# Linear half of the experts' first bias: from a TensorE matmul to a row read back from DRAM and added by VectorE

## What is computed

```python
def expert_block(args):
    xblk, e = args
    hh = xblk @ w1[e] + b1[e]                      # 1024 -> 2048
    glu = jnp.minimum(hh[:, :D_FF], SWIGLU_LIMIT)  # the gate's half
    lin = jnp.clip(hh[:, D_FF:], -SWIGLU_LIMIT, SWIGLU_LIMIT)  # the linear half
    act = glu * jax.nn.sigmoid(SWIGLU_ALPHA * glu) * (lin + 1.0)
    return act @ w2[e] + b2[e]
```

## Time and profile before

| what | value |
|---|---|
| median of 3 runs | 2273.63 us |
| the profiled execution, its own time | 2272.34 us |
| its span, from the first to the last instruction | 2270.5 us |
| granted TensorE clock, mean | 0.997 |
| TensorE busy | 98% of the span |
| VectorE busy | 78% of the span |
| ScalarE busy | 55% of the span |
| bytes moved by DMA | 542.98 MB |

### The profile page before, as it was taken

One profiled execution on the slowest core, in us unless ns is written; L12 is line 12 of the kernel. 1 busy time (PEld: TensorE's weight loads), 2 busy tenths in 40 slices (PEclk: granted clock), 3 DMA queues, 4 the chain that ended last, 5 costly groups with the idle time before them and its releaser, 6 DMA issues.

```text
span 2270.5 us, 30667 instructions
## 1 busy us (share of the span) xinstructions
PE 2235.7 (98%) x10681; PEld 1828.9 (81%) x10681; DVE 1768.0 (78%) x1652; ACT 1238.4 (55%) x1154; POOL 450.8 (20%) x422
## 2 busy tenths in 40 slices
PE   7999999999999999999999999999999999999997
PEld 3888888888887887888788888888888888888886
DVE  6756655555656766757899999999999999999996
ACT  6322132222225624632777777777777777777774
POOL 3000000000221131102522222232222222223222
PEclk9999999999999999999999999999999999999999
DMA  8322323131321121146899999999999999999995
GB/s 301 121 93 93 99 87 130 57 131 57 106 96 38 38 75 38 57 149 216 317 359 370 372 371 379 382 369 369 382 363 379 365 366 381 375 369 380 378 368 192
DMA packets 135517, 542.98 MB, mean 239 GB/s; under 512 B 16132, under 2 KB 24468, under 8 KB 101391
## 3 DMA queue, kind: packets, MB, share of 16 engines
q1 hardware_dynamic: 123192, 516.30, 60.2%
q0 software_dynamic: 11952, 21.44, 4.0%
q10 hardware_dynamic: 296, 4.21, 0.5%
HBM read 533.79 MB, written 26.38 MB: 247 GB/s over the span
## 4 chain that ended last, share of the span: by engine, by line
PE 95%; DMA 2%; DVE 1%; POOL 1%; issue 1%; ACT 0%; POOLq 0%; SPq 0%; DVEq 0%
PE ps L2263 90%; PE ps L2819 1%; PE ps L2831 1%; PE ps L2610 1%; DMA ar<-h_d,ar 1%; POOL list_d L865 1%; DMA ar<-in_ctx 0%; PE ps L2555 0%; DMA out_x<-ar,cur 0%; DMA raw<-in_w_mod 0%; PE ps L2501 0%; PE ps L2375 0%; DVE nmx L1866 0%; ACT hhi L1017 0%; PE ps L2708 0%
## 5 line engine op out<-in xcount | busy, mean ns | idle before, releaser
L2263 PE MATMUL ps<-whi,yhi 128*128 128x512 f32 x1072 | 346.4, 393 | 0.1
L2263 PE MATMUL ps<-hhi,yhi 128*128 128x512 f32 x1072 | 342.5, 389 | 0.0
L2083 DVE TENSOR_TENSOR hlo<-raw,hhi 128x2048 fp32r<-128x2048 f32 x132 | 302.7, 2294 | 47.2 <-ACT hhi L1324 47.2
L1324 ACT ACTIVATE whi<-raw 128x2048 fp32r<-128x2048 f32 x132 | 253.4, 1920 | 98.9 <-PE ps L2263 98.9
L2083 DVE TENSOR_TENSOR wlo<-raw,whi 128x2048 fp32r<-128x2048 f32 x132 | 298.8, 2284 | 3.3 <-ACT whi L1324 1.9
L1324 ACT ACTIVATE hhi<-raw 128x2048 fp32r<-128x2048 f32 x132 | 253.1, 1918 | 76.5 <-PE ps L2263 76.4
L1441 DVE TENSOR_TENSOR wlo<-raw,whi 128x2048 fp32r<-128x2048 f32 x56 | 128.2, 2289 | 159.4 <-ACT whi L986 159.4
L2263 PEld LDWEIGHTS ps<-whi,yhi 128*128 128x128 f32 x1072 | 201.2, 188 | 53.9 <-issue 12.1
L2263 PEld LDWEIGHTS ps<-hhi,yhi 128*128 128x128 f32 x1072 | 201.2, 188 | 41.8
L2263 PE MATMUL ps<-whi,hhi 128*128 128x512 f32 x592 | 233.3, 394 | 0.0
L2263 PE MATMUL ps<-whi,hlo 128*128 128x512 f32 x592 | 230.8, 390 | 0.0
(11 more groups left out here) (355 smaller groups left out, 4457.3 us busy)
## 6 DMA issues: line engine op xcount, KB each, us to landing
raw<-in_exp_w SPq DMA_DIRECT2D x264, 1024.0 KB, 8.3
ar<-in_exp_w SPq DMA_DIRECT2D x132, 1024.0 KB
raw<-in_w_in SPq DMA_DIRECT2D x44, 1024.0 KB, 5.1
raw<-in_w_mod SPq DMA_DIRECT2D x22, 1024.0 KB, 6.2
raw<-in_w_br_ret SPq DMA_DIRECT2D x8, 1024.0 KB, 5.3
ar<-in_x SPq DMA_DIRECT2D x8, 512.0 KB, 7.8
raw<-in_w_br_diff SPq DMA_DIRECT2D x4, 1024.0 KB, 5.2
raw<-in_w_out SPq DMA_DIRECT2D x4, 1024.0 KB, 10.7
```

Of the source, the lines that this page charges most:

```text
L1324: act.activation(e_whi[j % ESPL], e_raw[s], ACT.Copy).then_inc(e_hi, 1)
L2083: V.tensor_tensor(e_wlo[j % ESPL], e_raw[s], e_whi[j % ESPL].bitcast(F32), ALU.subtract).then_inc(e_lo, 1)
L2263: return pe.matmul(out, lhsT, rhs, start=start, stop=stop, skip_group_check=skip)
```

## The change

The linear half of the bias no longer goes through TensorE. During setup, ScalarE adds 1 to it and writes it to DRAM (`acc_d`, one row of 1024 floats for each expert). For every item SP reads the expert's row back, copied to all 128 partitions (`load_linear_bias`, 512 KB), and VectorE adds it to the linear half when it reads PSUM; the clip becomes an instruction of its own, on SBUF. Of the four bias matmuls the two for the gate's half stay, in rows 0 to 63 and 64 to 127. The PSUM banks of the linear half are now started by the first weight matmul.

```diff
+A_LIN, A_LSRC = A_TH, A_BSRC + COL
+BIASES = 6
...
-                sp.dma_start(F(A_BSRC, D)[32 * r:32 * r + 32, :], a["exp_b1"][:, r // 2 * D:(r // 2 + 1) * D]).then_inc(b_loaded, 16)
+                sp.dma_start(F(A_BSRC, COL)[32 * r:32 * r + 32, :],
+                             a["exp_b1"][:, r // 2 * COL:(r // 2 + 1) * COL]).then_inc(b_loaded, 16)
+            for r in range(2):
+                sp.dma_start(F(A_LSRC, COL)[32 * r:32 * r + 32, :],
+                             a["exp_b1"][:, D + r * COL:D + (r + 1) * COL]).then_inc(b_loaded, 16)
...
+            def load_linear_bias(e, i):
+
+                if not isinstance(i, int):
+                    sp.wait_ge(moe_step, i * 2)
+                sp.dma_start(F(A_LIN, D), acc_d[one(e), :].broadcast_to((P, D))).then_inc(b_loaded, 16)
...
+            sp.wait_ge(stored, 16 * (LT + 2))
+            load_linear_bias(0, 0)
             with sp.Fori(1, N_EXPERTS) as i:
                 for j in range(FIRST):
                     load_w1(i, i, j)
+                load_linear_bias(i, i)
                 for k in range(MOE_N - FIRST):
                     load_w2(i - 1, i, FIRST + k, k)
...
-            act.wait_ge(b_loaded, 64)
-            bsrc = F(A_BSRC, D)
-            act.activation(bsrc[64:128, :], bsrc[64:128, :], ACT.Identity, bias=ones[64:128, 0:1]).then_inc(bias_hi, 1)
+            act.wait_ge(b_loaded, 16 * BIASES)
+            linear = F(A_LSRC, COL)[0:2 * N_EXPERTS, :]
+            act.activation(linear, linear, ACT.Identity, bias=ones[0:2 * N_EXPERTS, 0:1]).then_inc(bias_hi, 1)
+            act.activation(bias, F(A_BSRC, COL), ACT.Copy).then_inc(bias_hi, 1)
             act.wait_ge(bias_hi, 1)
-            for q in range(2):
-                act.activation(bias[q], bsrc[:, q * COL:(q + 1) * COL], ACT.Copy).then_inc(bias_hi, 1)
+            for r in range(2):
+                act.dma_start(acc_d[0:N_EXPERTS, r * COL:(r + 1) * COL],
+                              linear[32 * r:32 * r + 32, :]).then_inc(stored, 16)
...
             def activate(i, between):
 
+                dve.wait_ge(b_loaded, i * 16 + 16 * (BIASES + 1))
                 dve.wait_ge(e_used, chunk(i, FIRST - 1) + 1)
-                V.tensor_scalar(ac, psf[:, 4 * COL:6 * COL], 1.0 - LIMIT, 1.0 + LIMIT, ALU.max,
-                                ALU.min).then_inc(moe_step, 1)
+                V.tensor_tensor(ac, psf[:, 4 * COL:6 * COL], F(A_LIN, D), ALU.add).then_inc(moe_step, 1)
                 between()
+                dve.wait_ge(moe_step, i * 2 + 1)
+                V.tensor_scalar(ac, ac, 1.0 - LIMIT, 1.0 + LIMIT, ALU.max, ALU.min).then_inc(moe_step, 1)
                 dve.wait_ge(glu_done, i + 1)
-                dve.wait_ge(moe_step, i + 1)
+                dve.wait_ge(moe_step, i * 2 + 2)
...
                 def add_bias():
-                    for b in (0, 2, 1, 3):
-                        r = slice(b // 2 * 64, b // 2 * 64 + 64)
-                        last = mm(ps[:, 2 + b, :], sel[r, :], bias[b % 2][r], not late, False)
+                    for b in range(2):
+                        r = slice(b * 64, b * 64 + 64)
+                        last = mm(ps[:, 2 + b, :], sel[r, :], bias[r], not late, False)
                     last.then_inc(sel_used, 1)
...
-                        mm(o, xthi[:, kk, :], wh, late and kk == 0, False)
+                        mm(o, xthi[:, kk, :], wh, kk == 0 and (late or b > 1), False)
```

More of the change, by code:

```diff
@@ L474, in build @@
         hh = [h[:, :, :].rearrange("p a b -> p (a b)").rearrange("p (s k n) -> p s k n", s=3, k=KH) for h in (hhi, hlo)]
-        bias = [hh[0][:, 2, q, :] for q in range(2)]
+        bias = hh[0][:, 2, 0, :]
         sel = hh[0][:, 2, 2, 0:P]
@@ L749, in extra @@
                     load_w1(e, i, j)
+                load_linear_bias(e, i)
                 for k in range(MOE_N - FIRST):
@@ L762, in _ @@
             sp.wait_ge(last_added, 32)
-            sp.wait_ge(stored, 16 * LT)
+            sp.wait_ge(stored, 16 * (LT + 2))
         @block.gpsimd
@@ L953, in _ @@
             pool.sem_inc(pool_m, 3)
-            pool.wait_ge(stored, 16 * LT)
+            pool.wait_ge(stored, 16 * (LT + 2))
             for t in range(LT):
@@ L1394, in bias_out @@
                 if t == 0:
-                    act.wait_ge(stored, 16 * LT)
+                    act.wait_ge(stored, 16 * (LT + 2))
                 act.wait_ge(gb_done, t + 1)
@@ L2218, in _ @@
             dve.wait_ge(ones_made, 5)
[L2219 to L2222, removed]
-                                       op1=ALU.add).then_inc(bias_lo, 1)
+            dve.wait_ge(bias_hi, 2)
+            V.scalar_tensor_tensor(out=bias, in0=bias.bitcast(F32), scalar=low_rows[:, 0:1],
+                                   in1=F(A_BSRC, COL), op0=ALU.mult, op1=ALU.add).then_inc(bias_lo, 1)
             dve.wait_ge(gb_hi, 2)
@@ L2852, in up @@
                         pe.wait_ge(xt_lo, 2)
-                        pe.wait_ge(bias_lo, 2)
+                        pe.wait_ge(bias_lo, 1)
                         add_bias()
```

## The result

The changed kernel takes **2278.43 us** (median of 13 runs, 2275.80 to 2281.08) against 2272.50 for the kernel before on the same chip (13 runs, 2272.01 to 2274.12): ratio 1.0024, 95% interval 1.0017 to 1.0032. It is slower by 5.9 us. The profiled execution took 2278.16 us with a span of 2276.4, against 2272.34 and 2270.5 before. The granted clock was 1.00 throughout the expert stage before. After the change it fell to 0.50 twice there, for 3.4 us each time.

The account below looks back on a forecast made before the run. TensorE, busy 98% of the span, was taken as the bound. Its saving of -10.6 us and +16.7 for late loads gave +6.1, on the median of 2273.63 rounded 2280 us; range 2262 to 2297 (forecast's own 2275 to 2300).

Parts of the forecast that it names:

- TensorE, -10.6 us: Expert stage: two of four bias matmuls per item removed, 0.33 us an item, -10.6 us over 32 items (-7.3 to -14.5).
- The lower end: Smallest saving forecast for the removed bias matmuls: one matmul's time, 0.227 us an item, -7.3 us in all.
- Late loads, +16.7 us: Expert stage's weight queue: 19.5 us growth plus 7.4 for whole-row adds, less 10.2 of cushion, lost by TensorE.
- a reserve of 1.2: Weight queue: while loads queue, the DMA engines work off 1.2 us more than an item brings.
- a price of 1.5: Time of all 16 DMA engines for each item's added 512 KB bias load: 1.5 us, between 1.24 and 2.15.
- cushion: Lateness of loads absorbed before TensorE waits: landings growing from 5.5 to 12.1 us, plus 3.6 of low-part lead, 10.2 us.
- the lower end of 1.24: Lowest price of the added bias load, at the 421 GB/s of weight loads alone with a full queue: 1.24 us.
- Cost: nothing for TensorE: VectorE's sum and separate clip add 0.81 us an item, covered by its 2.39 us idle time, costing TensorE nothing.
- Rival 3: Expert stage: VectorE becomes the bound above 2.06 us added, TensorE saves nothing, about 2276 us; chance 0.04.
- Rival 1: Expert stage: the loads stay hidden, leaving TensorE's saving of 10.6 us alone, about 2264 us; chance 0.32.
- Setup: nothing: Before the loop: ScalarE's halved table copy and two small stores, for which SP waits, cost nothing.
- What would show it: Expected trace signs in the expert stage: periods of 34.97, later 35.5 us or more, landings beyond 12, waits for loads.

## Why the prediction was right or wrong

The forecast was 2280 us, with a loss to late loads that outweighs TensorE's saving; measured were 2278.4. On the span it gave +6.1 and the trace shows +5.9. The number and the sign hold, and loads are late as forecast. But two terms were too large by almost the same amount, which is luck, and one step failed: late loads alone cost 7.1 us, as much as TensorE saves (7.3), and the kernel with the load alone is as fast as the one before (2272.79 against 2273.01). That the changed kernel is slower takes VectorE's added work on top.

- **TensorE, -10.6 us: too large.** Measured -7.3 (matmuls alone). The step taken at half of the four matmuls' 0.67 us was wrong in what it halved. From the first bias matmul to the second weight matmul it was 0.67 + 0.33 = 1.00 us and is 0.43 + 0.34 = 0.77: one matmul's time less. The remaining pair costs 0.43, not 0.33: the second pair had added 0.24 to it. The lower end, and the rule of the Trainium skill's page "TensorEngine Tiling (Array Packing)" beside it, was right to a tenth: -7.3.
- **Late loads, +16.7 us: too large.** The load alone costs 7.1 us. The mechanism was right (ScalarE waits 51.6 us for loads), the working was not. It let the queue grow by 0.63 us in every item, from a reserve of 1.2 and a price of 1.5. No such growth is there. Of its cushion no row shows the 3.6 us by which a low part stands ready: `up` waits for it before the bias matmuls, at 1612.25 and not at 1612.6, and it had ended at 1609.40, so it is 2.85.

The DMA queue of the weights from 1300 to 2200 us in the changed kernel, as in the earlier trace rows, and its median landings of whole weight blocks (last column):

```profile
q1 hardware_dynamic: 60882, 332.85, 92.8%
...
raw<-in_exp_w SPq DMA_DIRECT2D x204, 1024.0 KB, 10.2
ar<-in_exp_w SPq DMA_DIRECT2D x100, 1024.0 KB, 11.1
```

12.5 MB more, as much as 24 rows of bias, raised the packets' share from 91.7 to 92.8%: 9.9 us of all engines, 0.4 us a row, a third of the lower end of 1.24. By these numbers the packets' time held some waiting, which the added bytes filled: 384 GB/s went through instead of 371, 390 in an ordinary item. The share of packet time was no measure of what an item needs, and a drain of 1.2 us an item none of what the engines could do more. The queue still came down after each rise: the median landing is 12.2 us in the window from 1354.2 and 8.7 in that from 1495.4, against 11.8 and 7.1. It stood some 2 us higher in the median (10.2 against 8.3 from 1300 to 2200 us), and the loss came in five items, two after the first whole-row add and three after the third. That part the forecast had priced at 7.4 us.
- **"Cost: nothing for TensorE" (VectorE, +0.81 us an item): the step that failed.** The sizes were close: the sum is 1.22 us instead of 1.28 and the clip 0.71 instead of 0.75, +0.70 in place of +0.81. By itself it costs 1.0 us, in the last item. But the step asked who waits for VectorE's results, and not who needs VectorE to pause. GpSimd does, for its scatter, and the selection matrix is queued behind that. With the load this costs about 5 us more (uncertain by as much), of which moving the matrix gave 3 back. Without any load one more clip than VectorE's gaps can bear costs 24 us. The idle time of 2.39 us an item was counted as free cover. Without the load that was so down to 1.0 us left (34.03 busy of 35.07 in an item of the run with two clips), and no longer at 0.5 (34.6 with three); with late loads it was not so even at 1.6 (35.10 - 33.51 in the item of the second stretch above), since after a late load VectorE has no pauses for a while whatever its mean.
- **Rival 3, VectorE becomes the bound, from 2.06 us added:** at 2.1 us added, three clips, the time is 2291.9, and 2269.7 with the matrix earlier. The point of decision was right by chance; the wait was another.
- **Rival 1, the loads stay hidden, 2264:** this is the kernel with the matmuls alone or with four row groups (2265.7 and 2265.9). With the load it did not happen. The high bandwidth that it built on did: 384 to 390 GB/s.
- **Setup: nothing.** Item 1 starts 0.9 us later. In the experiments' traces the first bias matmul of item 1 starts between 1118.01 and 1120.98 (before 1118.02, after 1118.96), in no order of what was changed, so this can't be told from chance.
- **What would show it.** Early items at 34.97: they ran at 35.07. A second half at 35.5 or more: no, single long items, 13 and 25. Landings above 12 us: 13.2 us after the first whole-row adds. ScalarE's waits of tens of us: yes. TensorE idle for low parts: 1.3 us in two items, and 5.5 for the selection matrix in three. Bias matmuls as one pair of about 0.33 us: 0.43. What the list didn't have is the clock, whose two falls cost 3.2 us.

The total was right by luck: -10.6 and +16.7 were each too large in size, by 3.3 and 3.5 us (13.2 us measured in place of 16.7, and in the 13.2 is all that VectorE's work added).

The Trainium skill's page "SBUF — State Buffer" (Who interferes with whom) says that a VectorE instruction with two SBUF inputs contends with a GpSimd instruction that reads SBUF. The traces agree for the matrix and the copy. Where VectorE stands idle or reads PSUM, they take 0.29 and 0.18 us in the changed kernel. Started beside a low part they last until it ends, up to 2.3 us, in the kernel before as well. The same section infers that such an instruction leaves descriptor generation (the part of issuing a transfer that GpSimd does itself) alone; the scatter's 2.8 to 16.0 us here say otherwise, and the measurement decides. The scatter also reads its row numbers (`cur`) from SBUF; which of its parts is held up, no run here shows. That a port is what GpSimd waits for is the page's reading; the runs show only that its instruction lasts until VectorE pauses or reads PSUM.

## What to carry to other kernels

Before idle time of an engine is counted as cover, look at what runs on the engines beside it during that work, and what is queued behind that: here VectorE's pauses were GpSimd's time to issue its scatter, and a matrix for TensorE stood behind a wait for the scatter's landing. Order the program of a helper engine so that what others need comes before its own waits; here one step moved gave 22 us where VectorE was full, and about 3 in the changed kernel. Count a wait of TensorE at more than its length where the clock may fall behind it: 2.56 us of waiting cost 4.1. And a saving that comes from packing small matmuls can be had by packing them tighter, before work is moved to engines and queues that have only a few per cent of room.

## What the runs showed that was not expected

- GpSimd's scatter of 128 rows lasts 2.8 us, or 5.0, 7.2, 9.4, 11.6, 13.8, 16.0: steps of one VectorE low part (2.2 us). In the two that were followed it ended 1.5 to 1.6 us after VectorE's first gap (of 0.2 us, with three clips) or its first instruction that reads PSUM (in the changed kernel).
- TensorE's granted clock fell from 1.00 to 0.50 for 3.4 us after idle times of 2.56 us (twice, changed kernel), 2.02 (load alone) and 3.94 (three clips), and the item grew by another 1.6 us each time. Of eight idle times of 1.7 us (three clips), one was followed by such a fall.
- A fixed load of 512 KB per item cost 2.4 us at a period of 35.30 us and 7.1 us at 35.07.
- Two matmuls of 64 rows and four of 32 rows both took 0.43 us until a whole-height matmul started; four of 64 rows took 0.67.
- The clip from SBUF takes 0.71 us for 1,024 columns, the same from PSUM 1.22; a sum of PSUM and SBUF takes 1.22 as well.
